# Decode attention units: the head's mix is made token by token and divided by the row sums afterwards, and the steps of head and softmax are placed anew

## The reference, cut to what matters

```
# prompt, for each head: q (512 x 96), k (512 x 96), v (512 x 64)
sc  = (q_nope @ k_nope.T + q_rope @ k_rope.T) * ATTN_SCALE
sc  = where(key_pos <= q_pos, sc, -big)
p   = softmax(sc)                 # exp(sc - row max) / row sum
out = p @ v
# decode, for each sequence: lat (4097 x 128), kr (4097 x 32)
kv     = (lat @ w_ukv).reshape(n, 8, 64 + 64)
k_nope = rms_norm(kv[..., :64], k_nope_g)
sc     = (q_nope . k_nope + q_rope . kr) * ATTN_SCALE
out    = softmax(sc) @ kv[..., 64:]
```

## Time and profile before

| What | Value |
|---|---|
| Time, median of 3 runs | 1078.58 us (1077.5 to 1078.97) |
| Time of the profiled execution | 1072.7 us |
| Its span, first to last instruction | 1070.9 us |
| Busy share of the span | PE 89%, DVE 63%, ACT 47%, POOL 17% |
| Mean granted PE clock | 0.968 of full speed |
| Chain that ended last | PE 70%, DVE 12%, ACT 11% |

### The profile page before, as it was taken

One profiled execution on the slowest core, in us unless ns is written; L12 is line 12 of the kernel. 1 busy time (PEld: TensorE's weight loads), 2 busy tenths in 40 slices (PEclk: granted clock), 3 DMA queues, 4 the chain that ended last, 5 costly groups with the idle time before them and its releaser, 6 DMA issues.

```text
span 1070.9 us, 20298 instructions
## 1 busy us (share of the span) xinstructions
PE 957.9 (89%) x7860; PEld 878.3 (82%) x7860; DVE 673.3 (63%) x1597; ACT 506.6 (47%) x839; POOL 179.9 (17%) x186
## 2 busy tenths in 40 slices
PE   5699986789889897989889697999999999999997
PEld 3388864478778787878778597999999999999997
DVE  3693055777777677677767455777777777742312
ACT  2324461477676676767666442444444443331210
POOL 0021330123222222332221013000000000100000
PEclk9699996899999999999999899999999999999999
DMA  9966734000202020202200353124324322544202
GB/s 341 298 202 197 236 134 164 1 1 20 80 21 80 21 80 21 99 27 73 80 2 10 90 139 53 40 79 112 84 78 110 86 78 78 149 122 112 58 4 80
DMA packets 106288, 100.11 MB, mean 93 GB/s; under 512 B 7119, under 2 KB 94943, under 8 KB 104126
## 3 DMA queue, kind: packets, MB, share of 16 engines
q1 hardware_dynamic: 102422, 77.91, 25.0%
q0 software_dynamic: 3456, 20.97, 5.5%
q10 hardware_dynamic: 340, 0.27, 0.1%
HBM read 96.41 MB, written 2.94 MB: 93 GB/s over the span
## 4 chain that ended last, share of the span: by engine, by line
PE 70%; DVE 12%; ACT 11%; issue 4%; DMA 2%; SPq 0%; POOL 0%; ACTq 0%; DVEq 0%
PE ps L843 46%; PE ps L1200 11%; PE ps L838 4%; DVE FS L2082 2%; DMA RW<-w_ada 2%; PE ps L1135 2%; PE ps L1112 2%; ACT krT L1547 2%; ACT RB L1547 2%; PE ps L869 1%; PE ps L1158 1%; ACT RB L1506 1%; ACT qrot L1547 1%; PE ps L1195 1%; DVE prep L2046 1%
## 5 line engine op out<-in xcount | busy, mean ns | idle before, releaser
L843 PE MATMUL ps<-normed_high,up_weights_high 128*128 128x260 f32 x704 | 142.7, 284 | 3.5 <-DVE normed_low L1764 3.3
L843 PE MATMUL ps<-normed_high,up_weights_low 128*128 128x260 f32 x704 | 142.4, 284 | 0.0
L843 PE MATMUL ps<-normed_low,up_weights_high 128*128 128x260 f32 x704 | 142.3, 284 | 0.0
L801 POOL TENSOR_TENSOR latents_low<-RB,latents_high 128x512 fp32r<-128x512 f32 (+1 forms) x72 | 87.5, 1215 | 270.3 <-ACT latents_high L1507 269.9
L1200 PE MATMUL ps<-key_weights_high,latents_high 128*128 128x260 f32 x528 | 123.7, 316 | 0.4 <-ACT latents_high L1507 0.4
L843 PEld LDWEIGHTS ps<-normed_high,up_weights_high 128*128 128x128 f32 x704 | 109.2, 190 | 4.0 <-issue 3.3
L1604 ACT ACTIVATE up_weights_high<-RW 128x1024 fp32r<-128x1024 f32 x44 | 46.6, 1061 | 136.0 <-PE ps L843 133.6
L843 PEld LDWEIGHTS ps<-normed_high,up_weights_low 128*128 128x128 f32 x704 | 109.2, 189 | 0.0
L843 PEld LDWEIGHTS ps<-normed_low,up_weights_high 128*128 128x128 f32 x704 | 108.9, 189 | 0.0
L1200 PE MATMUL ps<-key_weights_low,latents_high 128*128 128x260 f32 x528 | 106.3, 282 | 0.0
L1200 PE MATMUL ps<-key_weights_high,latents_low 128*128 128x260 f32 x528 | 106.3, 282 | 0.0
(11 more groups left out here) (315 smaller groups left out, 2109.3 us busy)
## 6 DMA issues: line engine op xcount, KB each, us to landing
RW<-w_ada SPq DMA_DIRECT2D x24, 1024.0 KB, 7.3
RW<-w_up SPq DMA_DIRECT2D x44, 512.0 KB, 4.9
RW<-w_down SPq DMA_DIRECT2D x8, 1408.0 KB, 7.0
RW<-w_in SPq DMA_DIRECT2D x11, 512.0 KB, 7.9
RB<-w_o SPq DMA_DIRECT2D x8, 512.0 KB, 4.0
RB<-x_prompt SPq DMA_DIRECT2D x2, 1024.0 KB, 12.8
o_y_p<-RB SPq DMA_DIRECT2D x4, 512.0 KB
cst<-consts SPq DMA_DIRECT2D x1, 845.0 KB, 11.0
```

What stands on the lines that cost most here:

```text
L801: nc.gpsimd.tensor_tensor(latL[:, g % 3, c:4 * P], turned[:, g % 3, c:4 * P], latH[:, g % 3, c:4 * P].bitcast(F32), ALU.subtract).then_inc ...
L843: last = mm(ps[j % 4][rows[0]:rows[1], h, 0:H], lhsT, src[:, h * H:(h + 1) * H], start=start, stop=stop)
```

## The change

The mix of a head, before the change, multiplied normalised probabilities into a tile with the value dimension in the partitions. Now it multiplies the probabilities as the exponential leaves them into a tile with the tokens in the partitions, and DVE divides by the row sums when it takes the result out (`scaled_out`). Two heads lie side by side in that tile (`otk`), and after each odd head PE turns both at once (`turn_out`) and ACT copies them (`mixed`, in odd units alone). `norm_probs` is gone, and with it its semaphore. The two banks' jobs are dealt anew, and the steps of both chains stand at other places between the tiles on all four engines. The score copies (L2079, L2080) are on VectorE in both. The core of the diff (calls that only lost their bank number are left out):

```diff
-BANKS = (("qt", "mt", "mb", "s3", "s1", "p1", "mix"), ("kt", "s20", "p20", "pv", "p3"))
+BANKS = (("qt", "mt", "mb", "s3", "s1", "p3", "ot"),
+         ("kt", "s20", "p20", "pv", "p1", "mix"))
...
+        otk = prep[:, 16:16 + 4 * P].rearrange("p (a d) -> p a d", a=4)
...
@@ POOL
-                    if 0 < u < NS - 1 and g == 0:
+                    if 0 < u < NS - 1 and g == 1:
                         kfull(pool, key_job(u - 1, "t", NG - 1))
                         cached_keys((u + 1) % 2, u + 1)
...
-                    if 0 < u < NS - 1 and g == 4:
-                        bfull(pool, 1, "pv", u)
+                    if 0 < u < NS - 1 and g == 3:
+                        bfull(pool, "pv", u)
                         cached_latents((u + 1) % 2, u + 1)
@@ PE
             def head_mix(u):
-                r = VD * (u % 2)
+                for n in range(4):
+                    for a in range(n + 1):
+                        last = mm(bank("mix")[:, VD * n:VD * n + VD], hpt[:, a, P * n:P * n + P], vtok[:, a, VD * u:VD * u + VD],
+                                  start=(a == 0), stop=(a == n))
+                last.then_inc(is_full("mix"), 1)
+
+            def turn_out(u):
+
+                bclaim("ot", u)
+                bfree(pe, "mix", u)
                 for a in range(4):
-                    last = mm(bank(0)[r:r + VD, P * a:NP], vtok[:, a, VD * u:VD * u + VD], hpt[:, a, P * a:NP], start=(a == 0), stop=(a == 3))
-                last.then_inc(bank_full[0], 1)
+                    last = tr(bank("ot")[:, P * a:P * a + P], otk[:, a, :], P)
+                last.then_inc(is_full("ot"), 1)
...
-                        if (g, n) == (1, 1) and u > 0:
+                        if (g, n) == (1, 1):
+                            head_scores(u, "s20", (2, 0))
+                        if (g, n) == (1, 2) and u > 0:
                             turn_max(u)
-                        if (g, n) == (1, 2):
-                            head_scores(u, 1, "s20", (2, 0))
-                        if (g, n) == (2, 0) and u > 0:
+                        if (g, n) == (1, 3) and u > 0:
                             spread_max(u)
                         if (g, n) == (2, 2):
-                            head_scores(u, 0, "s3", (3,))
-                        if (g, n) == (3, 1):
-                            turn_probs(u, 1, "p20", (2, 0))
+                            head_scores(u, "s3", (3,))
+                        if (g, n) == (3, 2):
+                            turn_probs(u, "p20", "s20", (2, 0))
                         if (g, n) == (4, 0):
-                            head_scores(u, 0, "s1", (1,))
-                        if (g, n) == (4, 2) and u > 0:
+                            head_scores(u, "s1", (1,))
+                        if (g, n) == (4, 3) and u > 0:
                             pv(u)
-                        if (g, n) == (5, 2):
-                            turn_probs(u, 1, "p3", (3,))
-                        if (g, n) == (6, 0):
-                            turn_probs(u, 0, "p1", (1,))
-                        if (g, n) == (7, 1):
+                        if (g, n) == (5, 0):
+                            turn_probs(u, "p1", "s1", (1,))
+                        if (g, n) == (5, 3):
+                            turn_probs(u, "p3", "s3", (3,))
+                        if (g, n) == (6, 2):
                             head_mix(u)
+                        if (g, n) == (7, 2) and u % 2 == 1:
+                            turn_out(u)
@@ ACT
-                        if (g, n) == (0, 1) and u > 0:
+                        if (g, n) == (0, 0):
+                            head_in(u, "kt", headk, NOPE)
+                        if (g, n) == (0, 2):
+                            head_in(u, "qt", headq, QK)
+                        if (g, n) == (0, 3) and u > 0:
                             rstd_keys(u)
-                        if (g, n) == (0, 2):
-                            head_in(u, 0, "qt", headq, QK)
-                        if (g, n) == (0, 3):
-                            head_in(u, 1, "kt", headk, NOPE)
-                        if (g, n) == (2, 0):
-                            head_probs(u, 1, (2, 0))
-                        if (g, n) == (2, 3) and u > 0:
+                        if (g, n) == (2, 2):
+                            head_probs(u, "s20", (2, 0))
+                        if (g, n) == (3, 0) and u > 0:
                             probs(u)
-                        if (g, n) == (3, 1):
-                            head_probs(u, 0, (3,))
+                        if (g, n) == (3, 2):
+                            head_probs(u, "s3", (3,))
                         if (g, n) == (4, 2):
-                            head_probs(u, 0, (1,))
-                        if (g, n) == (7, 3):
+                            head_probs(u, "s1", (1,))
+                        if (g, n) == (7, 2) and u % 2 == 1:
                             mixed(u)
@@ DVE
-            def norm_probs(u, b, name, blocks):
-                    st.seq(V.reciprocal(rl[:, c:c + 1], l_[:, c:c + 1]))
-                    V.tensor_scalar(p, p, rl[:, c:c + 1], None, MUL).then_inc(s_pn, 1)
+            def scaled_out(u):
+
+                bfull(dve, "mix", u)
+                st.seq(V.reciprocal(rowl, l_))
+                V.tensor_tensor(otk[:, :, VD * (u % 2):VD * (u % 2) + VD], bank("mix")[:, 0:4 * VD].rearrange("p (a d) -> p a d", a=4),
+                                rowl.unsqueeze(2).to_broadcast([P, 4, VD]), MUL).then_inc(is_free("mix"), 1)
...
+                        if (g, n) == (1, 0) and u > 0:
+                            head_max(u)
                         if (g, n) == (1, 2) and u > 0:
-                            head_max(u)
+                            shift(u)
                         if (g, n) == (1, 3):
-                            row_max(u, 1, "s20", (2, 0))
-                        if (g, n) == (2, 1) and u > 0:
-                            shift(u)
+                            row_max(u, "s20", (2, 0))
                         if (g, n) == (2, 3):
-                            norm_probs(u, 1, "s20", (2, 0))
-                        if (g, n) == (3, 0):
-                            row_max(u, 0, "s3", (3,))
-                        if (g, n) == (3, 1) and u > 0:
+                            row_max(u, "s3", (3,))
+                        if (g, n) == (3, 2):
+                            turned_probs(u, "p20", (2, 0))
+                        if (g, n) == (3, 3) and u > 0:
                             prob_sums(u)
-                        if (g, n) == (3, 3):
-                            turned_probs(u, 1, "p20", (2, 0))
-                        if (g, n) == (4, 1):
-                            row_max(u, 0, "s1", (1,))
+                        if (g, n) == (4, 0):
+                            row_max(u, "s1", (1,))
+                        if (g, n) == (4, 2) and u > 0:
+                            finish(u)
                         if (g, n) == (4, 3):
-                            norm_probs(u, 0, "s3", (3,))
-                        if (g, n) == (5, 0) and u > 0:
-                            finish(u)
-                        if (g, n) == (5, 1):
-                            norm_probs(u, 0, "s1", (1,))
+                            turned_probs(u, "p1", (1,))
                         if (g, n) == (5, 3):
-                            turned_probs(u, 1, "p3", (3,))
-                        if (g, n) == (6, 2):
-                            turned_probs(u, 0, "p1", (1,))
-                        if (g, n) == (6, 3) and u < NS - 1:
+                            turned_probs(u, "p3", (3,))
+                        if (g, n) == (6, 1):
+                            scaled_out(u)
+                        if (g, n) == (8, 0) and u < NS - 1:
                             split_queries(u + 1)
```

More of the change, by code:

```diff
@@ L218 @@
 KEY_JOBS = UNIT * NS
[L219 removed]
+BANKS = (("qt", "mt", "mb", "s3", "s1", "p3", "ot"),
+         ("kt", "s20", "p20", "pv", "p1", "mix"))
+BANK = {name: b for b in range(2) for name in BANKS[b]}
 OF_FORMER = ("mt", "mb", "pv")
@@ L1111, in head_scores @@
                     w = P * (n + 1)
-                    last = mm(bank(b)[:, at:at + w], headq[0:QK, P * n:P * n + P], headk[0:QK, 0:w], start=True, stop=True)
+                    last = mm(bank(name)[:, at:at + w], headq[0:QK, P * n:P * n + P], headk[0:QK, 0:w], start=True, stop=True)
                     at += w
-                last.then_inc(bank_full[b], 1)
-            def turn_probs(u, b, name, blocks):
-                bclaim(b, name, u)
+                last.then_inc(is_full(name), 1)
@@ L1159, in pv @@
-                last.then_inc(bank_full[1], 1)
+                    last = mm(bank("pv")[r:r + GROUP, 0:KV], snd_all[e][:, HEADS * n:HEADS * n + GROUP], lat[e][:, n, :], start=(n < 4), stop=(n >= KTILES - 4))
+                last.then_inc(is_full("pv"), 1)
             def transposes(u, g):
```

155 lines of the change are left out of this document (80 added, 75 removed).

## The result

The changed kernel takes 1031.58 us (median of 4 runs, 1029.43 to 1033.47), against 1078.78 for the kernel before beside it on the same chip (1077.5 to 1083.32). The ratio is 0.9555, with a 95% interval of 0.9519 to 0.959: 47 us faster, where 36 was forecast. The direction was right, and so was the main cause: both placement waits are gone.

What follows compares the result with a forecast made beforehand. No engine is full; PE, ACT and DVE share three PSUM slots, with placement waits. Units: 10.2 + 15.8 + 17.05 = 43.05 against 47.89, 34 us over seven, 2 in the first: 1078.6 - 36 = 1043; range 1034 to 1064.

Steps and rivals of the forecast that it cites:

- stretch two: From DVE having the decode maxima to start of `pv`: 19.91 us falls to 15.8 as the s3 wait goes.
- stretch one: From a unit's first transposes to T0, when DVE has the decode maxima: 8.97 us grows to 10.2, for the split.
- stretch three: From start of `pv` to end of k32: 19.01 us falls to 17.05, with the mix at 1.46.
- the first unit: The unit without decode softmax, 44.09 us: gains 0.83 of the mix and half its full-slot waits, 2 us.
- I take the savings off the median: Whole kernel: savings from the profile (time 1072.7) are subtracted from the median 1078.58, some 5.9 us above it.
- some waiting stays: Between the decode maxima and `pv`: PE and DVE, nearly even over three slots, still wait; 15.8 us against bound 15.05.
- Both are hidden, since these engines are idle for over 10 us of a unit: From `pv` to k32: DVE's division replacing the rest of `norm_probs` (1.1 us) and ACT's changed copy cost no time.
- POOL and the loads: POOL's cached latents, issued earlier, delay the piece needed at k24: 4.7 us available, covered by half a microsecond; loads fit.
- Waits at full slots that stay: Rival, chance 0.14: each part of the unit comes out at its upper end, gain 1.8 us a unit, 1065.
- Loads late: Rival, chance 0.06: cached latents reach group 7's first transposes late, costing 2.9 us in six units, 1060.
- DVE and PE waiting for each other: Rival, chance 0.06: waits at `finish`, p1's copy, `scaled_out` and the split are not hidden; unit 49 us, 1087.
- Nothing comes of it: Rival, chance 0.04: each placement wait turns up in front of another step, 1078.6 us.

Runs made afterwards that it cites:

- e2: Changed kernel with the decode chain's steps on PE and DVE back at their old places: 1060.65 us, ratio 0.9796.
- e3: Kernel before with only the decode chain's steps on PE and DVE moved to the changed kernel's places: 1058.12 us, ratio 0.9783.
- e4: Kernel before with only the token-major mix, scaled_out and turn_out, without norm_probs, other steps at old places: 1085.25 us, ratio 1.0028.
- e6: Changed kernel with the old mix and its normalisation at the new places, p1's turn two tiles later: 1044.7 us, ratio 0.9654.
- e8: Changed kernel with the old mix, p20 one tile later, prob_sums one earlier, split_queries back behind k27: 1032.64 us, ratio 0.9562.
- e7: Kernel before, unchanged, run once more for a second profile: 1080.37 us.
- early-split kernel: Changed kernel with the next unit's split_queries back behind k27 on DVE: 1020.84 and 1021.3 us, ratios 0.9427 and 0.9456.

## Why the prediction was right or wrong, point by point

The forecast was 1043 and the changed kernel took 1031.6, 11.4 less. By profile, that is: 4.6 in what the runs have above their profiles, 6.2 in the seven later units, 2.7 in the first, less 1.1 and 1.2 by which units start and the tail ends later: 11.2. By the windows of one unit the 6.2 are 6.9 of stretch two and 2.0 of stretch one, less 2.7 of stretch three. The offset (4.6), stretch two (6.9) and the first unit (2.7) are each larger than the 2.4 us by which the range was missed.

**"I take the savings off the median": this step failed.** The median of before lies 5.9 above its profile, and that of the changed kernel 1.3 above its own. I took that 5.9 for a constant offset. The second profile of before lies 7.7 above the first, and of that 4.7 are in its last two units: behind the waits for the maxima and for s3 the clock falls, and in one of them DVE's instruction of 1.34 us comes first. In both profiles of the changed kernel no later unit is longer than its like. The other 3.0 lie in a stage that the change leaves alone, and the timed runs of the changed kernel still differ by 4 us. That the change removed the 4.6 is argued from two profiles of each kernel and not measured by itself.

**Stretch one was right.** Forecast 10.2, measured 9.92 by T0: it moved back by 0.95, which I had called the least. The wait for the split is 1.05, where I had 1.3, and it is paid: moved back, it gives 8 to 11 us, 1.3 a unit.

**Stretch two was right in its cause; "some waiting stays" failed.** Both placement waits went. I took 15.8, with some waits at full slots left, and called 15.05 the lower bound. By T0 it took 14.82, which over seven units is 6.9 us, the largest single term of the miss. "With two engines that are nearly even over three slots some waiting stays" was the wrong choice; none stayed. And 15.05 was no bound: it was made from PE's busy time in a window, 15.97, which has modelled ends of products in it, and I treated them as work. The last pair of products ahead of the wait for s3 shows it:

```profile
365.55 0.41 PE L1200 MATMUL ps<-key_weights_high,latents_low 128*128 128x260 f32 x2
```

It is counted for 0.41 us, up to where the idle 2.57 begins, while such pairs follow each other at 0.24; this comes once for each wait. (That it is the whole of the 0.23 was not measured by itself.)

**Stretch three was right but for one price.** Forecast 17.05, measured 17.60 in a unit with `turn_out`, 17.4 as a mean. The 0.55 behind `finish` went, `turn_out` is four transposes in 0.35 (I had counted 0.43). The mis-sized term is the mix: 2.15 us and not 1.46. I took 0.073 for an instruction, by the nearest row below (L1195), and it was 0.1075, the upper row's 0.108. The Trainium skill's page "TensorE: Matmul & The Clock Gate", section "LDWEIGHTS (loading the stationary operand)", by which each load of 128 columns would take 107 ns, gave an estimate of 2.13; the trace agrees with it, at 2.15 and at 4.38 for twice as many. I had set this rule aside because of one row whose two passes stand between products of another kind, and where I had divided a start-to-start time of 0.14 by two. A pair that stands alone doesn't show the rate of a row of twenty. So the new mix saves PE 0.14 us, and `turn_out` costs 0.18, more than that.

**The first unit was mis-sized.** I gave it 2 us and it gained 4.7. With the decode chain put back it still takes 39.28 us (e2), and in the kernel before with the chain moved 43.38 (e3), so the gain is mostly of the new mix with the head's new places and not of the chain. The new mix alone at the old places gives 0.3 (43.75 in e4, at a granted clock of 0.94 where the kernel before had 0.97) and the new places with the old mix 2.8 (41.34 in e6), each to within the 0.8 that one kernel's first unit differs by. PE's idle time in it went from 3.28 us to 0.05: "half of its waits at full slots" should have been all of them, and 1.5 more are in busy time, which has modelled ends, and are not accounted for.

**"Both are hidden, since these engines are idle for over 10 us of a unit": this step failed.** I priced what the new mix takes off DVE at nothing: in stretch two it only lowered DVE's sum to 14.3, below PE's. The new mix is worth nothing at the old places (e4, no gain) and 11 to 13 us in the new ones (e6, e8), though PE's work is the same. Idle time of an engine over a unit is no cover: the normalisation of s20 stands between the exponentials and PE's turn of p20, and it counts whenever PE arrives there first. In the kernel before, PE has lost 1.4 and 2.6 us at other places by then, and shows no wait at p20. With the decode chain moved (e3) the same row waits 0.60, with all places new (e6) 1.04, and with p20 a tile later (e8) the old mix still falls 0.66 behind. As far as it was tested, this is why the parts don't add up: chain alone 24, mix alone 0, the new places with the old mix 37, all together 47. How much of the 11 us is DVE's time as such is open; the comparison changes ACT's copy and PE's mix with it.

**POOL and the loads** were covered as counted: no row of PE in groups 6 and 7 has a bracket by POOL or a DMA.

**The rivals.** Waits at full slots that stay: refuted, none is left. Loads late: refuted. DVE and PE waiting for each other: DVE's waits came out at 0.90, 0.83 and 1.41, 3.1 together, where I had given 1.5, 0.6 and 1.5, and the slots hide all three; the only one paid is that at the border. Nothing comes of it: refuted.

**What stays open**: which of the head's placements in groups 3 to 7 bring how much of the 13 us that lie between the chain alone (1058) and all places with the old mix (1045); they were only run together. Whether the normalisation at another place would bring the old mix level with the new one, no run shows.

## What to carry to other kernels

When engines hand work over through a few slots, first take away the waits that are placements, read at PE's rows that have a bracket (here 6.2 us of them left a unit, 1.1 came in, and the unit became 5.7 shorter). A step taken out of a chain on an engine that isn't the bound may be worth nothing before that and a per cent after, so measure it in the tight version. And a median above its profile is a quantity of its own: ask what it is made of before it is carried over, and price a row of short products by another row of the same loads, not by a pair that stands alone.

## What was not expected of the hardware

A product of 64 moving columns with a 128-column operand to load takes 0.1075 us in a row of twenty, as a transpose with 128 columns does (0.108); half the columns bring nothing.

The clock: the same wait of 2.56 us before s3 is followed by a granted clock of 1.00 in most units and by a fall in some (a mean of 0.81 over 6 us in e7; in e4 a mean of 0.67 over 8 us, with pairs at 0.43 us for 0.24 while the clock is at its lower level, 1.2 GHz). Long waits are not needed for it: in e2 it falls in all four odd units behind waits of 1.58 and 1.68 us, and in no even one, with the same waits. The changed and the early-split kernel, which have neither wait, show no fall in a later unit. Over all chips and runs the kernel before took 1073 to 1089 us, and up to 1091 in three runs, the changed one 1028 to 1033 and the early-split one 1018 to 1024. What decides in which unit the clock falls, no run here shows.

One DVE instruction of 8 columns took 1.33 to 1.34 us in place of 0.23, four times in the 28 later units that have it 0.05 us ahead of POOL's product of 1.3 us (none in the first profile of before and in e3, one in e7, three in e4), and never where POOL starts 0.25 behind. Each time PE's wait for the maxima grew by 1.1 us.
